# The scan's four turned operands: 64x64 products with the unit matrix, or whole transposes of one side-by-side buffer

## What is computed

```python
def step(S, inp):
    r_t, w_t, k_t, v_t, kk_t, kka_t = inp
    sa = jnp.einsum("bhvk,bhk->bhv", S, kk_t)
    S = S * w_t[:, :, None, :] - sa[..., None] * kka_t[:, :, None, :] + v_t[..., None] * k_t[:, :, None, :]
    return S, jnp.einsum("bhvk,bhk->bhv", S, r_t)
s_final, ys = lax.scan(step, wkv0.astype(jnp.float32), xs)
```

## Time and profile before

| | |
|---|---|
| time, median of 3 runs | 4391.52 us (4388.79 to 4394.6) |
| span of the profiled execution | 4412.3 us |
| mean granted TensorE clock | 0.907 of full |
| TensorE busy, share of the span | 87% |
| VectorE busy | 69% |
| GpSimd busy | 41% |
| scan of `e_` | about 296 to 525 us |
| scan of `l_` | about 1504 to 2128 us |
| experts, to the end | from about 2970 us |

### The profile page before, as it was taken

How to read it: one execution, slowest core, us unless ns; L and a number is a source line. 1 busy time by engine, 2 the same in 40 slices (tenths; PEclk the granted TensorE clock), 3 DMA queues, 4 the chain that set the end, 5 groups by cost and what they waited for, 6 DMA issues and landing times. The chain is left out here.

```text
span 4412.3 us, 71906 instructions
## 1 busy us (share of the span) xinstructions
PE 3824.5 (87%) x28135; PEld 2549.9 (58%) x28135; DVE 3027.1 (69%) x5958; ACT 957.2 (22%) x2001; POOL 1819.1 (41%) x1489
## 2 busy tenths in 40 slices
PE   7877888899999788888788886668999999999998
PEld 6766765555555577787665464564444444454444
DVE  0454422598688467767786478876889788977777
ACT  1332221010233323222451013770000000000001
POOL 0007000076223033332225207735666566666764
PEclk9998888899999899898679997679999999999999
DMA  7543443499577466766549633459999999999998
GB/s 176 164 153 102 134 162 142 149 381 402 189 253 268 172 211 205 256 206 204 191 135 384 243 141 52 97 158 382 406 397 394 402 406 404 390 403 407 403 406 317
DMA packets 434556, 1152.50 MB, mean 261 GB/s; under 512 B 80734, under 2 KB 175523, under 8 KB 430851
## 3 DMA queue, kind: packets, MB, share of 16 engines
q0 software_dynamic: 207216, 687.87, 42.9%
q1 hardware_dynamic: 194276, 419.98, 26.4%
q10 hardware_dynamic: 32727, 40.05, 2.6%
HBM read 1044.67 MB, written 113.65 MB: 263 GB/s over the span
## 5 line engine op out<-in xcount | busy, mean ns | idle before, releaser
L2781 PE MATMUL x_sps<-c_big,l_c_wo 128*128 128x384 f32 x2048 | 692.8, 501 | 72.7 <-DMA l_c_wo<-u_cols 69.4
L385 POOL DMA_INDIRECT l_w_ring<-u_rows,k_eidx x256 | 295.6, 1155 | 944.6 <-DVE l_w_dots L441 398.1
L2789 PE MATMUL x_vps<-l_c_v,x_w 128*128 128x512 f32 x1536 | 662.3, 592 | 3.0 <-DVE x_w L2838 3.0
L385 POOL DMA_INDIRECT w_ring<-u_rows,k_eidx x384 | 481.2, 1253 | 433.2 <-DVE w_dots L441 264.7
L2781 PEld LDWEIGHTS x_sps<-c_big,l_c_wo 128*128 128x128 f32 x2048 | 400.6, 196 | 365.4 <-DMA l_c_wo<-u_cols 76.7
L458 DVE SCALAR_TENSOR_TENSOR l_c_share<-w_ring,w_wts,l_c_share 128x1024 f32<-128x1024 f32 x384 | 493.5, 1285 | 59.3 <-DMA w_ring<-v_rows,k_eidx 45.0
L2789 PEld LDWEIGHTS x_vps<-l_c_v,x_w 128*128 128x128 f32 x1536 | 291.7, 190 | 367.6 <-issue 358.3
L385 POOL DMA_INDIRECT w_ring<-v_rows,k_eidx x384 | 422.9, 1101 | 131.1 <-issue 119.9
L385 POOL DMA_INDIRECT l_w_ring<-v_rows,k_eidx x256 | 293.8, 1148 | 330.2 <-DVE l_w_yacc L458 264.9
L458 DVE SCALAR_TENSOR_TENSOR l_w_yacc<-l_w_ring,l_w_wts,l_w_yacc 128x1024 f32<-128x1024 f32 x256 | 328.9, 1285 | 31.7 <-DMA l_w_ring<-v_rows,k_eidx 21.3
L581 PE MATMUL l_pzp<-c_big,l_c_w 128*128 128x384 f32 x960 | 312.7, 488 | 17.6 <-DMA l_c_w<-w_tiles 17.6
(11 more groups left out here) (650 smaller groups left out, 6283.3 us busy)
## 6 DMA issues: line engine op xcount, KB each, us to landing
l_c_wo<-u_cols SPq DMA_DIRECT2D x128, 512.0 KB
l_c_v<-v_rows SPq DMA_DIRECT2D x128, 512.0 KB
e_c_w<-w_tiles SPq DMA_DIRECT2D x54, 512.0 KB, 3.7
l_c_w<-w_tiles SPq DMA_DIRECT2D x54, 512.0 KB
l_c_wo<-s_G SPq DMA_DIRECT2D x16, 1536.0 KB
s_rw<-l_q_out SPq DMA_DIRECT2D x48, 384.0 KB
s_G<-l_c_share ACTq DMA_DIRECT2D x8, 2048.0 KB
s_zT<-l_pz ACTq DMA_DIRECT2D x30, 384.0 KB
```

What stands on the lines that cost most here:

```text
L385: pool.indirect_dma_start(out=self.ring[:, r, :], out_offset=None, in_=self.A[table], in_offset=bass.IndirectOffsetOnAxis(ap=idx[:, s:s + ...
L2781: mm = pe.matmul(sps[n % 2][:, 0:ND * P], u[n % 4][:, k, :], hT[:, k, :], start=(k == 0), stop=(k == KT - 1))
L2789: mm = pe.matmul(vps[k][:, x * 512:(x + 1) * 512], w[:, e, k * P:(k + 1) * P], v[:, e, x * 512:(x + 1) * 512], start=(c == 0 and e == 0), ...
```

## The change

The four operands `vn`, `bn`, `kn`, `an` get a load of their own. A new buffer of `4 * n` columns (`by_token`, in `kept`) holds two of them on partitions 0 to 63 (`vn`, `kn`) and two on 64 to 127 (`bn`, `an`). Within one, each chunk has both heads side by side: 64 columns of head 0, then 64 of head 1. `load_turned(p)` fills it with eight DMAs, one for each operand and head, of 64 rows x `NC` chunks x 64 numbers; each run of 64 numbers (256 bytes) lands by itself. `ab`, `rbT` and the others are read as before from `rw`, which now holds four arrays. `R_ALPHA` is loaded twice, once for each buffer.

TensorE then makes one `transpose` for each chunk, 64 rows x 128 columns into 128 x 64, in place of two 64x64 products: 4 in `e_` and 12 in `l_` for a batch.

There is one such buffer, not one for each parity of the pair. So the load of pair `p` waits for `an` of pair `p - 1`, the last reader. The load of pair 1 stands behind `side.sp`; in turn `p` the load of pair `p + 2` stands behind the store of pair `p - 1`. GpSimd's wait ahead of the background gather is now for the new load of pair 0.

```diff
@@ scan_pairs: buffers
-        rw = [kept[:, 0:N_RW * n].rearrange("p (i t) -> p i t", i=N_RW), sb("r_in1", [P, N_RW, n])]
+        by_token = [kept[:, i * n:(i + 2) * n].rearrange("p (c h t) -> p c h t", h=2, t=CL) for i in (0, 2)]
+        turn_from = {"vn": by_token[0][0:HD], "bn": by_token[0][HD:P], "kn": by_token[1][0:HD], "an": by_token[1][HD:P]}
+        rw = [sb(f"r_in{j}", [P, N_OP, n]) for j in range(2)]
@@ scan_pairs: sync
             def load_early(p):
                 for i in FIRST_IN:
                     sp.dma_start(rw[p % 2][:, i, :], A["rw"][p, i, :, tokens]).then_inc(ab_in[p % 2], 16)
-                for i in THEN_IN:
-                    sp.dma_start(rw[p % 2][:, i, :], A["rw"][p, i, :, tokens]).then_inc(rw_in[p % 2], 16)
+
+            def load_turned(p):
+                for name, i in THEN_IN:
+                    for h in range(2):
+                        sp.dma_start(turn_from[name][:, :, h, :], chunks(A["rw"][p, i, half(h), tokens])).then_inc(rw_in, 16)
...
             load_early(0)
+            load_turned(0)
             load_late(0)
...
             side.sp(sp)
+            sp.wait_ge(pe_prep, PP.after("an", 0))
+            load_turned(1)
             sp.wait_ge(pe_prep, PP.after("rkT", 0))
             load_early(2)
             for p in range(NPAIR):
...
                 if p:
                     store(p - 1)
                     load_gb(p)
+                if p + 2 < NPAIR:
+                    sp.wait_ge(pe_prep, PP.after("an", p + 1))
+                    load_turned(p + 2)
                 if p + 3 < NPAIR:
                     sp.wait_ge(pe_prep, PP.after("rkT", p + 1))
                     load_early(p + 3)
@@ scan_pairs: tensor, prep_batch
                 if name == "vn":
-                    pe.wait_ge(rw_in[j], 48 * (p // 2 + 1))
+                    pe.wait_ge(rw_in, 32 * len(THEN_IN) * (p + 1))
...
                 for c in range(NC):
+                    if name in turn_from:
+                        rows = half(name in ("bn", "an"))
+                        mm = pe.transpose(ps[slot_of[name]][:, col(c)], turn_from[name][:, c].rearrange("f h t -> f (h t)"), ident[rows, rows])
+                        continue
                     for h in range(2):
-                        mm = pe.matmul(ps[slot_of[name]][half(h), col(c)], lhsT[half(h), col(c)],
-                                       ident[half(h), half(h)] if rhs is None else rhs[half(h), col(c)],
-                                       start=True, stop=True)
+                        mm = pe.matmul(ps[slot_of[name]][half(h), col(c)], lhsT[half(h), col(c)], rhs[half(h), col(c)], start=True, stop=True)
@@ scan_pairs: gpsimd
-            pool.wait_ge(rw_in[0], 48)
+            pool.wait_ge(rw_in, 32 * len(THEN_IN))
```

More of the change, by code:

```diff
@@ L47 @@
 (R_ALPHA, R_BETA, R_KAPPA, R_RHO, R_BETAE, R_KAPPAE, R_V) = range(7)
-N_RW = 7
+N_RW, N_OP = 7, 4
 PH, NKEY, TOPK = 8, 128, 16
@@ L1034, in attend_tiles @@
 def attend_tiles(A, pt):
-    o, out = (N_RW + 6) * pt.n if pt.first else 0, {}
+    o, out = (N_OP + 6) * pt.n if pt.first else 0, {}
     for name, dims in (("kT", (2, WIN + pt.n)), ("vT", (2, WIN + pt.n)), ("q0", (KT, WIN)), ("q1", (KT, WIN)),
@@ L1046, in kept_floats @@
     need = 2 * 2 * (WIN + pt.n) + 2 * KT * WIN + NH * 2 * WIN + NH + NB
-    return (N_RW + 6) * pt.n + need if pt.first else max((N_RW + 6) * pt.n, need)
+    return (N_OP + 6) * pt.n + need if pt.first else max((N_OP + 6) * pt.n, need)
 def load_attend(sp, A, pt, to, kv_sem, sem):
@@ L1117, in scan_pairs @@
         kept = A["sb_kept"]
-        part = lambda i: kept[:, (N_RW + i) * n:(N_RW + i + 1) * n]
-        rw = [kept[:, 0:N_RW * n].rearrange("p (i t) -> p i t", i=N_RW), sb("r_in1", [P, N_RW, n])]
+        part = lambda i: kept[:, (N_OP + i) * n:(N_OP + i + 1) * n]
+        by_token = [kept[:, i * n:(i + 2) * n].rearrange("p (c h t) -> p c h t", h=2, t=CL) for i in (0, 2)]
+        turn_from = {"vn": by_token[0][0:HD], "bn": by_token[0][HD:P], "kn": by_token[1][0:HD], "an": by_token[1][HD:P]}
+        rw = [sb(f"r_in{j}", [P, N_OP, n]) for j in range(2)]
         dend = two("r_dend", [P, NC])
@@ L1139, in scan_pairs @@
         const_in = sem("r_const_in")
-        ab_in, rw_in, rho_in, y_out = [[sem(f"r_{x}{j}") for j in range(2)] for x in ("ab_in", "rw_in", "rho_in", "y_out")]
+        ab_in, rho_in, y_out = [[sem(f"r_{x}{j}") for j in range(2)] for x in ("ab_in", "rho_in", "y_out")]
+        rw_in = sem("r_rw_in")
         att_in, kv_in, prm_in = sem("r_att_in"), sem("r_kv_in"), sem("r_prm_in")
@@ L1158, in scan_pairs @@
         tokens = slice(pt.t0, pt.t0 + n)
-        FIRST_IN, THEN_IN = (R_ALPHA, R_BETA, R_KAPPA), (R_V, R_BETAE, R_KAPPAE)
-        assert len({*FIRST_IN, *THEN_IN, R_RHO}) == N_RW
+        FIRST_IN, THEN_IN = (R_ALPHA, R_BETA, R_KAPPA), (("vn", R_V), ("bn", R_BETAE), ("kn", R_KAPPAE), ("an", R_ALPHA))
+        assert {*FIRST_IN, R_RHO} == set(range(N_OP)) and list(fill.values())[:4] == ["vn", "bn", "kn", "an"]
         def state(c, p, o):
@@ L1231, in prep_batch @@
                 name = order[g]
-                r = [rw[j][:, i, :] for i in range(N_RW)]
+                r = [rw[j][:, i, :] for i in range(N_OP)]
                 if name == "ab":
@@ L1247, in prep_batch @@
                     f"P{l}": (Pt[a], Pn[a], got), f"PT{l}": (Pn[a], Pt[a], got), f"X{l}": (Pn[b], X, (f"P{l}", f"X{l - 1}")),
-                    "vn": (r[R_V], None, ()), "bn": (r[R_BETAE], None, ()), "kn": (r[R_KAPPAE], None, ()), "an": (r[R_ALPHA], None, ()),
+                    "vn": (None, None, ()), "bn": (None, None, ()), "kn": (None, None, ()), "an": (None, None, ()),
                     "rbT": (r[R_BETA], r[R_RHO], ()), "rkT": (r[R_KAPPA], r[R_RHO], ()),
```

## The result

The changed kernel took 4439.4 us (median of 4 runs, 4428.2 to 4452.3) against 4390.2 us (4 runs of the kernel before beside them, 4383.6 to 4394.6): ratio 1.0111, interval 1.009 to 1.0132, 49 us slower. Forecast were 22 us more, 4413.5 us. The direction was right, the size 22 us of 49. That 4439.4 us still lies in the range of 4383 to 4440 us is luck: its upper end had been set for the slow weight load, which did not come. Two later measurements on other chips gave 1.0091 (1.0058 to 1.0125) and 1.0116 (1.009 to 1.0142), so 39 to 51 us on a kernel of some 4400.

A forecast was written before the change was run, and what follows sets the result against it. TensorE was taken as busiest in both scans, in a chain alternating with VectorE. +19.5 (first delay) + 16 (five stalls) - 13.5 (`l_`) = +22 us on 4391.5 gave 4413.5 us; range 4383 to 4440 us.

The forecast's parts named there:

- slow weight load: Rival: each transpose costs 0.11 us, so +5 us in `l_` and +5 more in `e_`, 4437 us; chance 0.12.
- The long wait in turn 0: `e_`: pair 1's load, now behind the decode loads, makes `vn` start 22.3 us late and turn 1 21.5 us late.
- the transposed batch: TensorE: 0.057 us a transpose; a batch in `l_` takes 0.95 us against 1.40, in `e_` 0.49 against 0.46.
- nothing late in `l_`: Loads in `l_`: eight issues take 9 us, doubled if the gather interferes, yet stay hidden by at least 13 us.
- the GpSimd lock: `e_` beside decode work: GpSimd operations exclude VectorE's two-SBUF-input steps; their 17.4 us cost becomes 15.4 after the shift.
- Five stalls: 3.5 + 2.9 + 2.7 + 3.3 + 3.5 = 16 us: `e_`, loads of pairs 3 to 7: `vn` waits for eight issues behind the store, whole on the chain, 16 us.
- Turn 2 is thus about 19.5 us late: `e_`: turn 1's 21.5 us delay, less what returns at the GpSimd lock, costs 19.5 us; ends +4 and +26.
- Sum -13.5 us: `l_`: shorter batches and fewer TensorE stops save 1.8 us in each of 7 turns, plus 1 us ahead of turn 0.
- Carrying the profile's distance to the median over: Whole kernel: runs' median taken as 20.8 us below the profiled span, so 4391.5 + 22 = 4413.5 us.
- Small stalls: Rival: first delay costs +4 us, five stalls 1 us each, `l_` gives -20; 4381 us in all; chance 0.10.
- Small pieces: Rival, `l_`: pieces crowd the DMA engines, TensorE's stops grow by half, the gain is gone; 4431 us; chance 0.13.
- The clock in `l_`: Rival: transposed batches pull TensorE to its lower clock, 14 us on the chain; 4427 us; chance 0.05.

The follow-up runs named there:

- loop_e: Changed kernel with the turned load of pair p+2 ahead of the store, gate and bonus in `e_` alone; 1.0028 against before, +12 us.
- rows: Changed kernel whose turned loads copy whole rows (1 KB pieces in `e_`, 3 KB in `l_`, for 256 B), output not the reference's; 1.0105 against before, +46 us.
- loop_fix: Changed kernel with the turned load of pair p+2 ahead of the store, gate and bonus in both parts; 1.0045 against before.
- after_again: The changed kernel, unchanged, measured again on another chip with a second profile; 1.0091 against before.
- late_sp: Kernel before with transposes in `l_` alone, and pair 2's loads in both parts issued ahead of the decode loads; 1.0 against before.
- dbl: Changed kernel with a second turned buffer in `e_`, so turned loads are issued where the kernel before issued its operands; 1.0009 against before, +4 us.
- late_only: Kernel before with transposes and the single turned buffer in `l_` alone; 0.997 against before, -13 us.

## Why the prediction was right or wrong

**Right:** slower, by the single buffer. The long wait in turn 0 for the turned load, behind the decode loads; five waits in the turns behind it; the transposed batch (0.88 us for 0.95, a transpose every 0.062 us for 0.057); nothing late in `l_` (four waits of 2.5 us in all at line 1267), though the eight issues there took 10 to 25 us, where I had 9, or 18 beside the gather; the GpSimd lock shifting and giving part of the first delay back.

**The step that failed most: "Five stalls: 3.5 + 2.9 + 2.7 + 3.3 + 3.5 = 16 us".** They cost 34 us (`loop_e` against `rows`, timed; 33 us in the `e_` scans of `loop_fix` and `after_again`). The mechanism held, the load behind the tail, the store and its own issues; the term was mis-sized. By turns: the first costs 9 us (turn 2, 36.6 us on average in five profiles for 27.2 in `loop_e` and `loop_fix`), the other four 25 (118.4 us for 93.0, the mean of eight profiles with products). The waits alone are 28 to 31 us, and the lower clock behind them adds some 2; some 4 us of the four later turns have no name here. Two numbers in the step were wrong. "Eight issues at 0.47 us" came from rows with three issues of whole rows; eight in a row take 0.61 to 0.77 us, with small pieces or large. And the first of the five, 10.5 us, was taken for one like the others: it follows the locked stretch, its `yb` is late and its issues take 1.15 us each (why the issues are slow there is open). The upper end I had given was 5 us a stall, 25 us; even that was short.

**"Turn 2 is thus about 19.5 us late".** With the five stalls gone and the first delay left (`loop_e`, `loop_fix`), `e_` takes 249.4 and 249.0 us against a mean of 239.0: 10 us. The delay of turn 0 was a little over the forecast (a wait of 24.8 us for 22.3, the turn 25.5 us longer for 21.5). But before itself lost time in turns 1 and 2: in eight profiles with products the first three turns took 90 to 112 us, 104 on average, and the profile I read, with 90, was the luckiest of them. There VectorE's long steps took 17.7 us beyond their usual 0.45 each; in the eight it is 18 to 27 us, 23 on average, and 8 to 12 in the eight with the late first load. So on average 13 us of the delay of 25 come back at the lock, where I had 2. I priced the lock on one execution.

**"Sum -13.5 us" for `l_`.** Timed alone: -13, +1 and -7.5 us on three chips, a mean of -6.5 (`late_sp`, with moved loads, 0 on a fourth); in the profiles -8.4, with the doubt stated there. The batches are shorter by what was forecast or a little more (0.5 us for 0.45), and the stops without a named wait fall from 30.7 to 28.6 us over the whole scan, about the tenth I had counted (at the preparation's batches from turn 0 on, from 19 to 13). TensorE is busy for 497 us instead of 512. But in the same profiles, on the slower chips, its waits for VectorE's state (`l_r_ST` at line 1296) grow from 36 to 43 us. About half of the 16 us that TensorE gains it spends there: `vn`, `bn` and `kn` do not all count whole. This is read from the waits, not tested; and in the four profiles with transposes on faster chips these waits are 34 to 35 us, as in the one with products there (35.6). Of the turn, 1.0 us is won (72.7 to 71.7 us, means of four and eight profiles), where 1.8 were forecast.

**The sum.** 34 + 10 - 8 = 36 us by these parts, or 50 - 6.5 = 43.5 by the two halves timed alone, against 39, 49 and 51 measured in three sets. The 7.5 us between the two sums are of the size of the intervals and not explained, and neither is why 49 and 51 were measured; that `dbl` is still 17 us slower than `late_only` says that `e_` loses something by time that its profiles do not show. Carrying the profile's distance to the median over was right for the whole. It hid that in the scans this execution was off both ways: `e_` 11 us short of the mean of its kind and, as an estimate, `l_` some 32 us over (620.5 against 579.8, the mean of the four with transposes on faster chips, and 8 more).

**The rivals.** Small stalls: out. Slow weight load: out, though its total (4437) was nearest. Small pieces: against before the stops of TensorE fell, where this rival had them grow by half, and `e_` is indifferent to the pieces. But against the same kernel with larger pieces they cost some 8 us in `l_` (`rows`), so the rival had a true part; and `loop_fix`, which moves the load in `l_`, has 12 to 29 us of stops (see above). The clock in `l_`: out, its time at the lower level was 134 to 174 us in the scans with products and 124 to 172 us in those with transposes. The clock behind the stalls of `e_` was named only in their upper end.

**Which version is best.** Transposes in `l_` alone: 0.997, 1.0003 and 0.9983 on three chips, against before. It beats the changed kernel by 1.1% on the chip that ran both, and before by 0.15% on average, about the half-width of one interval; two of the three intervals lie under 1.

## What to carry to other kernels

When a change halves a buffer, ask for each reload what its issue now waits for and what stands ahead of it on its queue, and price it with the count of issues in a row, not with the mean of a short group. A long block of issues in one queue (here 30 us of decode loads) is a wall: moving one load ahead of it pushes the next behind it. A saving on the busiest engine can be spent waiting for the next engine's result: look for the wait that grows. Read a stretch with a lock or a clock in it from several executions before its time goes into a sum. And compare each profiled execution with the median of its kernel's runs: here they lay up to 21 us over it and 11 us under it, more than most of the differences that the profiles were to explain.

## What the runs showed of the hardware

- SyncE's issues of eight DMAs to 64 partitions took 0.65 to 0.77 us each in turns 3 to 6 of `e_` with 256 byte pieces and 0.61 to 0.73 with 1 KB pieces (`rows`); in turn 2, 0.9 to 1.2 us with small pieces and 0.82 with large. In `l_` they took 1.2 to 3.1 us each with 768 pieces of 256 bytes, and 0.6 to 0.8 with pieces of 3 KB.
- Around the end of a pause of 4.6 us (510.8 to 515.4) the granted clock was 0.50 for 6.8 us, from 514.6 to 521.4, and TensorE was busy from 515.4 on.
- Five long VectorE steps with both inputs in SBUF, three before and two after, each ended 0.3 us behind a GpSimd operation. In twenty profiles the long steps beside the decode work took 8 to 27 us in all beyond their usual 0.45 each, by where they fell.
- The time of the same code scatters by execution: `l_` had between 124 and 174 us at the lower clock, `e_` from 227 to 248 us in all. Between chips `l_` with transposes took 578 to 582 or 599 to 610 us, at about the same time at the lower clock (148 to 162 us against 124 to 172). What makes that difference is open.
- TensorE's stops without a named wait in `l_` rose from 12 to 29 us when only the place of a load with 6144 small pieces in SyncE's queue changed, and they were 10.9 us over the scan with 3 KB pieces where three kernels with small pieces on the same chip had 18.9 to 23.0. Both point to TensorE's instruction stream being held up by that traffic. This was not isolated.
